# Moving the eight loads of x from one DMA queue to another at the start of a two-layer kernel

## The reference, cut to what matters

```python
h = _rmsnorm(x, norm_pre[i, 0])
proj = h @ w_in                      # 2048 x 10304: z, xs, B, C and dt of a state-space mixer
z, xbc, dt = jnp.split(proj, [SSD_D_INNER, SSD_D_INNER + SSD_CONV_DIM], axis=-1)
...                                  # mixer, cross attention, FFN, then the whole second block
```

## Time and profile before

| | |
|---|---|
| median of 3 runs | 2713.67 us (2711.70 to 2715.04) |
| the profiled execution's own time | 2714.08 us |
| its span in the trace | 2712.5 us |
| PE busy | 2678.1 us, 99% |
| DVE busy | 1736.5 us, 64% |
| ACT busy | 1337.3 us, 49% |
| x pieces | 8 DMAs of 256 KB |
| unit 0 weight pieces | 8 DMAs of 256 KB and 4 of 128 KB |

### The profile page before, as it was taken

The page is one execution under the profiler, slowest core; times in us unless marked ns, Lnnn a source line. Parts: engine busy times, 40 slices in busy tenths (PEclk is TensorE's granted clock), DMA queues, the critical chain, the costliest instruction groups (busy, mean ns, idle before and its releaser), DMA issues.

```text
span 2712.5 us, 37724 instructions
## 1 busy us (share of the span) xinstructions
PE 2678.1 (99%) x13921; PEld 2278.6 (84%) x13921; DVE 1736.5 (64%) x2133; ACT 1337.3 (49%) x1659; POOL 155.2 (6%) x130
## 2 busy tenths in 40 slices
PE   7999999999999999999999999999999999999998
PEld 6888888888778888888888887888888888888887
DVE  6777777754666767666744475644576766676444
ACT  5555555533566554555544464443465455545433
POOL 2311111100000000000000010000000000000000
PEclk9999999999999999999999999999999999999999
DMA  7555555565453555555555565434555555555552
GB/s 236 179 179 187 184 171 187 199 244 190 155 200 126 205 197 186 186 190 193 195 200 197 186 215 187 140 128 164 189 186 190 186 199 187 197 186 204 199 187 107
DMA packets 223163, 503.41 MB, mean 186 GB/s; under 512 B 15374, under 2 KB 50474, under 8 KB 202992
## 3 DMA queue, kind: packets, MB, share of 16 engines
q1 hardware_dynamic: 218160, 476.81, 52.2%
q0 software_dynamic: 4464, 24.99, 2.6%
q10 hardware_dynamic: 464, 0.59, 0.1%
HBM read 498.07 MB, written 4.28 MB: 185 GB/s over the span
## 4 chain that ended last, share of the span: by engine, by line
PE 95%; DVE 2%; issue 1%; ACT 1%; DMA 0%; SPq 0%; DVEq 0%; POOLq 0%; POOL 0%; ACTq 0%
PE PB L1214 14%; PE T L1214 13%; PE T L1522 12%; PE PB L1522 11%; PE PB L1168 9%; PE PB L1170 9%; PE PB L1169 9%; PE T L1525 6%; PE PB L1525 6%; PE T L1400 1%; PE T L1324 1%; DVE hT L1781 1%; DVE w_lo L1752 1%; PE T L1456 0%; DMA x<-in_x_dram 0%
## 5 line engine op out<-in xcount | busy, mean ns | idle before, releaser
L1752 DVE TENSOR_TENSOR w_lo<-raw,w_hi 128x2048 fp32r<-128x2048 f32 (+3 forms) x468 | 1037.6, 2224 | 598.4 <-ACT w_hi L714 596.5
L714 ACT ACTIVATE w_hi<-raw 128x2048 fp32r<-128x2048 f32 (+3 forms) x468 | 868.8, 1859 | 894.4 <-PE T L1214 384.6
L1168 PE MATMUL PB<-w_hi,hT 128*128 128x512 f32 (+3 forms) x1280 | 485.3, 379 | 5.4 <-DVE hT L1781 3.4
L1522 PE MATMUL T<-hT,w_hi 128*128 128x512 f32 x1408 | 489.7, 391 | 0.0
L1170 PE MATMUL PB<-w_hi,hT 128*128 128x512 f32 (+3 forms) x1280 | 471.3, 368 | 0.0
L1169 PE MATMUL PB<-w_lo,hT 128*128 128x512 f32 (+3 forms) x1280 | 471.1, 368 | 0.0
L1522 PE MATMUL PB<-hT,w_hi 128*128 128x512 f32 x1280 | 444.6, 391 | 0.0
L1525 PE MATMUL T<-hT,w_lo 128*128 128x256 f32 x1408 | 394.3, 280 | 0.0
L1525 PE MATMUL PB<-hT,w_lo 128*128 128x256 f32 x1280 | 358.4, 280 | 0.0
L1522 PEld LDWEIGHTS T<-hT,w_hi 128*128 128x128 f32 x1408 | 263.4, 187 | 58.0
L1214 PE MATMUL PB<-w_hi,hT 128*128 128x512 f32 x1120 | 305.2, 392 | 6.6 <-issue 3.0
(11 more groups left out here) (286 smaller groups left out, 2036.8 us busy)
## 6 DMA issues: line engine op xcount, KB each, us to landing
raw<-in_ffn_w_up_dram SPq DMA_DIRECT2D x88, 1024.0 KB, 5.1
raw<-in_w_up_dram SPq DMA_DIRECT2D x88, 1024.0 KB, 5.0
raw<-in_ssd_w_in_dram SPq DMA_DIRECT2D x64, 1024.0 KB, 5.2
raw<-in_ffn_w_down_dram SPq DMA_DIRECT2D x44, 1024.0 KB, 4.8
raw<-in_w_down_dram SPq DMA_DIRECT2D x44, 1024.0 KB, 4.8
raw<-in_w_in_dram SPq DMA_DIRECT2D x40, 1024.0 KB, 5.1
raw<-in_ssd_w_out_dram SPq DMA_DIRECT2D x32, 1024.0 KB, 4.8
raw<-in_ssd_w_in_dram SPq DMA_DIRECT2D x64, 256.0 KB, 3.2
```

Source lines behind the costliest of these rows:

```text
L714: nc.scalar.activation(dst, src, ACT.Copy).then_inc(hi_ready, 1)
L1168: nc.tensor.matmul(o, h, wh[:, c, :], start=(j == first and c == 0), stop=False)
L1522: ins = nc.tensor.matmul(banks[f][:, :], wh[:, c, s], both, start=(k == 0), stop=False)
L1752: V.tensor_tensor(dst, src, h.bitcast(F32), ALU.subtract).then_inc(lo_ready, 1)
```

## The change

x's eight pieces leave SP's queue. ACT issues them instead: both pieces of block 0 ahead of the three row loads, the six others behind them, all before ACT's first computing instruction. What waits for x (`x_landed`) stays as it is.

```diff
@@ SP
             for j in range(4):
-                for tt in range(TT):
-                    at = slice(j * BLK, (j + 1) * BLK)
-                    sp.dma_start(xt[:, tt, at], I["x"][0, tt * P:(tt + 1) * P, at]).then_inc(x_landed[j], 16)
                 load_bcd(j)
@@ ACT
+            def load_x(j):
+                for tt in range(TT):
+                    at = slice(j * BLK, (j + 1) * BLK)
+                    act.dma_start(xt[:, tt, at], I["x"][0, tt * P:(tt + 1) * P, at]).then_inc(x_landed[j], 16)
+
+            load_x(0)
             load_rows(act, True)
+            for j in range(1, 4):
+                load_x(j)
             act.wait_ge(cols_ready, 1)
```

## The result

| | before | after |
|---|---|---|
| median | 2714.16 us (20 runs, 2711.70 to 2717.05) | 2719.70 us (20 runs, 2716.84 to 2722.90) |
| profiled execution, span | 2712.5 us | 2718.4 us |
| PE busy | 2678.1 us | 2678.6 us |

The ratio after to before is 1.0021, 95% interval [1.0014, 1.0028]: slower, by 3.8 to 7.6 us. The forecast was 2714.8 us with a range to 2718.6; the time lies above it.

A forecast was written before the change was run, and what follows sets the result against it. PE was taken to bound the kernel (95% of the chain of waits), changeable only ahead of 48 us. Terms 0.0 + 1.1 = +1.1 us on the median 2713.67 gave 2714.8 us, range 2710.8 to 2718.6.

The forecast's parts named there:

- The rows stand behind x0: ACT's parameter rows, which start PE, are issued after two x pieces: +0.5 us, from no loss to +3.1.
- The wait for x1: PE's 3.89 us idle before x1 goes; quad 0 then waits for DVE's `w_lo`, so only -0.48 us.
- x2 and x3 ahead of W1: At quad 1, x2 and x3 on ACT's queue compete with W1's load and delay it: +1.1 us taken.
- +2.05: Upper case at quad 1: all of x2 and x3 passes before W1's last piece, 3.7 - 0.8 - 0.85 us.
- Eight more issues on ACT: ACT's eleven issues end at 5.8, its first work is at 9.50: 3.7 us of cover, nothing to pay.
- third rival: ACT caught in issuing past 9.50, delaying its table load and quad 0: slower by about 3.5 us, 2717.2; chance 0.15.
- The clock: PE's pace in the first products: no difference taken; ends 1.5 us won or 2.9 us lost.
- What carries on: From quad 1 to PE's wait at 48.05: a delay arrives in full, a gain until 1.76 us of waits are used.

The follow-up runs named there:

- e6: The changed kernel, but POOL issues none of its DMAs before ACT's rows have landed; 2716.5 us, ratio 1.0009 to before.
- e5: The changed kernel, but SP issues its first weight piece only when both pieces of x0 have landed; 2719.9 us, ratio 1.0021 to before.
- e9: The changed kernel, but POOL's DMAs wait for ACT's rows and SP's first weight piece waits for x0; 2720.3 us, ratio 1.0025 to before.
- e4: The kernel before, but POOL issues its three broadcasts behind its other parameter rows; 2713.4 us, ratio 1.0000 to before.
- e8: The kernel before, but x1 to x3 are issued by ACT behind its rows, x0 staying first on SP; 2717.7 us, ratio 1.0015 to before.
- e3: The changed kernel, but POOL issues its three broadcasts behind its other parameter rows; 2717.7 us, ratio 1.0013 to before.
- e7: The kernel before, but POOL issues none of its DMAs before ACT's rows have landed; 2714.0 us, ratio 1.0002 to before.
- e1: The changed kernel, but ACT issues its three parameter rows first and all eight pieces of x behind them; 2720.9 us, ratio 1.0029 to before.
- e11: The kernel before, but POOL issues its three broadcasts ahead of its first memset; 2715.2 us, ratio 1.0006 to before.

## Why the prediction was wrong

**The step that failed** is "The rows stand behind x0". I took +0.5 us for it, with +3.1 as the worst; it is +5.53. The cover for x0 was real: it came 2.2 us later, inside the 2.6 us of slack. But "the DMA engines are not full between 2 and 5 us", my reason for taking only the issue time, did not protect what followed it. And "no loss, if their 6.1 us was other traffic's doing" had it upside down: since other traffic governed the row's landing, being issued 1.2 us later (3.08 against 1.87) and behind x0 moved it into heavier traffic. The runs put that traffic to POOL's DMAs (3.9 us of the row's delay, e6) and to W0 beside it (3.4 us, e5); together, with e9's figures, 7.2 us, which are the 5.5 of the delay and the 1.7 by which e9's row is ahead of the kernel before. How much of it is the later issue and how much the bytes ahead in the queue, no run separates. I had the row for it: POOL's queue takes 74.3% of the engines between 6 and 9.5 us with only 55 packets. I used it to discount bandwidth and never asked which of the gating transfers would now fall into it.

**The upper bound** of that term was too low. It came from the nearest small DMA of another queue, W0's dt piece with 8.3 us. In the changed kernel the row took 10.4. A bound from a row of the old traffic did not hold for the new one.

**The wait for x1** went away as idle time, but not for the reason forecast: x1 did not come earlier (its first piece in at 13.6 and not ahead of 11, its second at 15.8 and not at 14.1); PE came later. The gain of 0.48 us never existed. I had set the chain's 16.13 beside the timeline's 15.65; by the timeline PE begins quad 0 at 15.80, 0.15 us after `w_lo`, in the kernel before already, and e4, with x1 2.3 us earlier, gained nothing beyond its row's 0.28.

**x2 and x3 ahead of W1**, my +1.1: W1's dt did come later, by 1.6 us (20.0 against 18.4), which lies between the 1.05 and 2.9 that I had before taking off the slack. It cost nothing, since the rows had delayed ACT's `w_hi` of W1 to 21.50 already. So the term is 0 in the sum. In e8, where the rows were on time, the same mechanism struck W0, and that kernel is 3.5 us slower. The mechanism was right; that it is paid for depends on what else is late, and I had not asked what x1 to x3 do to W0.

The rule that I had weighed there, of the Trainium skill's "DMA: Bandwidth & Descriptors", section "Issuing engines are not separate DMA queues", that all queues share the 16 engines and interleave, held for the sum: the DMA share of the first two windows is 0.83 and 1.09 now, and was 0.85 and 1.09. The +2.05 that I had worked out under it did not: the loss came from which transfer landed when, on which that section says nothing.

**Eight more issues on ACT**: I counted 3.7 us of cover and an end at 5.8; the end was 12.3. My third rival's mechanism happened, on the side where it decides, and still cost nothing, because PE released ACT only at 15.03. Its price was also summed wrongly: one more stall of 3.4 us on top of the 1.5 is 4.9 and not 3.4, which puts that rival's middle at 2718.0 and not at 2717.2.

**The clock** took hardly any part: 0.18 us between PE's first product (+5.53) and the transposes of x2 (26.78 against 21.07, +5.71). I had taken none.

**What carries on**: the delay arrived in full at the late wait (+5.70 with the same 1.12 us), as forecast. And the limit, that the change acts only ahead of 48 us, holds: from the late wait to the end of the span it is 2664.4 us before and 2664.7 now. With the terms as measured the sum is 5.53 for the rows, 0 for x1, 0 for W1 and 0.18 for the clock, 5.7 us; the medians differ by 5.5. The miss looks small, 1.1 us above the range, and 0.21% where 0.91 was given to a change within 0.2%. That it is so near is luck: the end of the range came from rival 3, which cost nothing, and the +1.1 of the forecast from W1, which was not paid.

## What to carry to other kernels

When a DMA is moved to another queue, ask for each small transfer that gates the start what will be in flight on all queues in the time in which it will now be served, not how many bytes stand ahead of it in its own queue. Moving bulk onto a second queue shares the engines between the bulk and the gate: here, with POOL's traffic left as it was, every arrangement with two bulk queues lost 3.5 to 7 us, whichever transfer was put second. And where an early start is won, check the pace of the first matmuls before counting it.

## What the runs showed of the hardware that I had not expected

POOL's broadcast loads can be very dear in engine time. In the changed kernel the queues' shares from 2 to 5 us (SP's, then ACT's) and from 6 to 9.5 us (POOL's) are:

```profile
q1 hardware_dynamic: 583, 0.29, 38.8%
q10 hardware_dynamic: 147, 0.27, 37.4%
...
q0 software_dynamic: 68, 0.08, 59.1%
```

68 packets took 59.1% of 16 engines for 3.5 us, 33.1 us, 0.49 us each; in the kernel before 55 took 74.3%, 0.76 us each. SP's 583 took 38.8% of 3 us, 0.03 us each. Three loads of 32 KB delayed a fourth by 3.2 us (e3 against the changed kernel). But they are not dear by themselves. In e7 the same three loads are issued from 6.9 us on, and POOL's queue has this from 9.5 to 14.5 us:

```profile
q0 software_dynamic: 162, 0.19, 19.3%
```

That is 0.10 us for a packet of much the same mean size. What makes the early ones five to eight times as dear is not shown.

A part of the spread of the runs arises far behind the change. At 537.00 in the profile before and at 539.98 in that of e8 PE ends an idle time of 3.01 us. The windows behind it, with the granted clock as the third number from the end, first before and then e8:

```profile
537.00:542.00 5.00, 5.00 (x18) 3.99 (x19) 5.00 (x6) 2.63 (x3) 0.00 (x0) 0.66 0.64 210
```

```profile
540.00:545.00 5.00, 5.00 (x26) 4.07 (x26) 5.00 (x6) 2.60 (x3) 0.00 (x0) 1.00 0.61 210
```

In the first the clock was at its lower level, 1.2 GHz, for a part of the stretch, in the second at the full 2.4 GHz level throughout. From the late wait to the end the kernel before took 2664.4 us and e8 2661.8. The other profiles agree: the four without a fall of the clock between 500 and 900 us (e1, e8, e9, e11) took 2661.6 to 2662.8 us for this part, the nine with one 2663.9 to 2666.7. So e8's profiled execution (2714.4) looks as good as before while its median is 3.5 us slower. A single execution can't judge a change of this size; the timeline ahead of 50 us can.
